# Hybrid attention and experts trunk, one core: the bias table laid out by position ahead of the launch, and the last experts in plain order

## What is computed

```python
for l in range(DEPTH):                                  # 2
    z = rms_norm(x, norm_mix[l]) @ w_in[l]              # 1024 x 3000
    ya = diff_attention(..., table[:, :4])              # 4 heads, two maps each
    yb = sparse_attention(..., table[:, 4:])            # 4 heads, the 64 best keys by an index score
    yc = mla(...)                                       # 4 heads, low-rank, no bias
    x = x + concat(ya, yb, yc) @ w_out[l]
    x = x + hier_moe(rms_norm(x, norm_ffn[l]), ...)     # 32 experts, each token goes to 2 of them
return rms_norm(x, norm_final)

def rel_bias(table, q0, n_keys):                        # table: 32 buckets x 8 heads, shared by the layers
    t, s = q0 + arange(128), arange(n_keys)
    return transpose(table[t5_bucket(s[None, :] - t[:, None])], (2, 0, 1))   # added to the logits
```

## Time and profile before

| | |
|---|---|
| runs | 1193.9, 1194.41, 1196.88 us; median 1194.41 |
| profiled execution | 1195.85 us; span 1194.0 us |
| busy | PE 933.0, PEld 583.0, DVE 334.3, ACT 196.0, POOL 18.4 us |
| DMA | 447.78 MB, mean 375 GB/s |
| granted TensorE clock | 0.903 of 2.4 GHz on the mean |
| chain that ended last | DMA 52%, PE 43%, ACT 1%, DVE 1%, issue 1% |

### The profile page before, as it was taken

One profiled execution on the slowest core, in us unless ns is written; L12 is line 12 of the kernel. 1 busy time (PEld: TensorE's weight loads), 2 busy tenths in 40 slices (PEclk: granted clock), 3 DMA queues, 4 the chain that ended last, 5 costly groups with the idle time before them and its releaser, 6 DMA issues.

```text
span 1194.0 us, 23281 instructions
## 1 busy us (share of the span) xinstructions
PE 933.0 (78%) x10312; PEld 583.0 (49%) x10317; DVE 334.3 (28%) x974; ACT 196.0 (16%) x529; POOL 18.4 (2%) x37
## 2 busy tenths in 40 slices
PE   9799999876667765776699999997776677648746
PEld 5577576443434343443368766664343334325423
DVE  3365662221102110211136465521111111111112
ACT  2134331010101010100022343311010001001102
POOL 1000000000000000000010000000000000000000
PEclk9899999898878788988799999999898888788878
DMA  8884499999999999999996165999999999999994
GB/s 322 358 305 139 186 375 424 425 431 429 427 432 425 431 426 431 424 430 430 423 426 226 63 260 213 388 427 431 428 429 425 432 427 430 429 428 427 429 431 176
DMA packets 35190, 447.78 MB, mean 375 GB/s; under 512 B 9584, under 2 KB 13072, under 8 KB 14992
## 3 DMA queue, kind: packets, MB, share of 16 engines
q1 hardware_dynamic: 32352, 443.49, 88.4%
q10 hardware_dynamic: 2736, 2.76, 0.7%
HBM read 442.57 MB, written 3.67 MB: 374 GB/s over the span
## 4 chain that ended last, share of the span: by engine, by line
DMA 52%; PE 43%; ACT 1%; issue 1%; DVE 1%; another core or an unknown queue 0%; POOL 0%; SPq 0%; ACTq 0%; POOLq 0%; DVEq 0%
DMA arena<-in_gate_up 22%; DMA xb<-in_w_down 14%; PE pv L1778 11%; PE pj L1399 7%; DMA ring<-in_w_down 7%; DMA ring<-in_gate_up 7%; PE tr L1800 5%; DMA bias_lines<-ring 2%; PE pj L1505 2%; PE pj L1405 2%; PE pj L1636 2%; PE pj L1810 2%; PE tr L1765 1%; PE pj L1611 1%; PE pj L1645 1%
## 5 line engine op out<-in xcount | busy, mean ns | idle before, releaser
L1778 PE MATMUL pv<-ring,xT 128*32 128x256 f32 x3072 | 222.4, 449 | 98.9 <-DMA ring<-in_gate_up 98.9
L1778 PEld LDWEIGHTS pv<-ring,xT 128*32 128x32 f32 x3072 | 107.8, 124 | 202.6 <-DMA ring<-in_gate_up 98.4
L1245 DVE TENSOR_SCALAR arena<-arena 128x128 f32<-128x128 f32 x64 | 14.5, 227 | 678.7 <-ACT arena L827 678.4
L1778 PE MATMUL pv<-arena,xT 128*32 128x256 f32 x1024 | 85.6, 502 | 67.6 <-DMA arena<-in_gate_up 67.6
L642 ACT ACTIVATE arena<-pv 128x256 f32<-128x256 f32 x64 | 24.5, 383 | 495.4 <-PE pv L1778 495.4
L1399 PE MATMUL pj<-xT,ring 128*128 128x256 f32 x448 | 101.9, 386 | 0.0
L1800 PE MATMUL tr<-ring,arena 128*32 128x256 f32 x1376 | 82.6, 380 | 15.0 <-issue 8.9
L1778 PEld LDWEIGHTS pv<-arena,xT 128*32 128x32 f32 x1024 | 39.0, 139 | 113.0 <-DMA arena<-in_gate_up 72.9
L1399 PEld LDWEIGHTS pj<-xT,ring 128*128 128x128 f32 x448 | 85.3, 193 | 13.7 <-issue 1.2
L1810 PE MATMUL pj<-arena 32*128 32x256 f32 x512 | 73.4, 403 | 8.1 <-ACT arena L642 8.1
L1810 PE MATMUL lg<-arena 32*128 32x256 f32 x512 | 73.4, 404 | 0.0
(11 more groups left out here) (238 smaller groups left out, 861.8 us busy)
## 6 DMA issues: line engine op xcount, KB each, us to landing
ring<-in_gate_up SPq DMA_DIRECT2D x42, 4096.0 KB, 48.5
ring<-in_w_down SPq DMA_DIRECT2D x40, 2048.0 KB, 41.3
arena<-in_gate_up SPq DMA_DIRECT2D x16, 4096.0 KB, 45.2
xb<-in_w_down SPq DMA_DIRECT2D x18, 2048.0 KB, 40.9
ring<-in_w_in_chunks SPq DMA_DIRECT2D x10, 2048.0 KB, 31.4
ring<-in_gate_up SPq DMA_DIRECT2D x10, 2048.0 KB, 8.7
ring<-in_w_out_halves SPq DMA_DIRECT2D x4, 2048.0 KB, 21.8
ring<-in_w_down SPq DMA_DIRECT2D x6, 1024.0 KB, 7.9
```

Of the source, the lines that this page charges most:

```text
L1778: ins = mm(gu_ps[i * CAP:(i + 1) * CAP, :], xg[:, j, c:c + CAP], w, start=(j == 0), stop=(j == KD - 1), tile_position=(0, i * CAP), skip_g ...
```

## The change

The bias is laid out by query and key for a tile of 128 queries ahead of the launch, as an input of 128 x 2048 numbers (`bias_rows`), like the weights, which already are laid out there. The kernel loads it in each layer on SP's queue between the input and output weights; GpSimd fills the masked corner in each layer; the one-hot matrix, the table product, the lines, their way through DRAM and the write-back are gone. In the last round of a layer, expert 30 is handled in the plain pattern, on TensorE and on ScalarE.

```diff
-    return (np.arange(REL_BUCKETS)[:, None] == bucket[None, :]).astype(np.float32)
+    return np.where(rel > 0, half, 0) + np.where(n < exact, n, np.minimum(large, half - 1))
 
 
 def loads_of(m):
...
-          gate_up_d, w_down, norm_final, consts_d, onehot_d, ffn_blocks_d, out_d):
-    lines_d = nc.dram_tensor("bias_lines", (8, P * LINE), F32, kind="Internal")
-    bias_d = nc.dram_tensor("bias_rows", (P, 8 * SEQ), F32, kind="Internal")
...
@@ -467,9 +457,6 @@
             def first_experts(l):
 
                 gu, down = gu_v[l * N_EXPERTS:], down_v[l * N_EXPERTS:]
-                if l < 1:
-                    sp.wait_ge(bias_ready, 1)
-                    sp.dma_start(bias_d[:, :], bias[:, 0:8, :].rearrange("p h k -> p (h k)")).then_inc(bias_out, 16)
                 sp.wait_ge(win_used[0], l + 1)
                 sp.wait_ge(win_used[1], l + 1)
                 sp.dma_start(gu_place[0], gu[0]).then_inc(gu_full[0], 16)
...
-                if l < 1:
-                    sp.wait_ge(bias_out, 16)
                 sp.dma_start(d_place[2][:, KE // 2:], down[2][:, KE // 2:]).then_inc(d_full[2], 16)
...
@@ -530,13 +515,9 @@
                         sp.dma_start(con[:, C_FIRST:], consts_d[:, C_FIRST:]).then_inc(more_consts_in, 16)
                     if l < 1 and i == 1:
                         load_small(sp, 0)
-                if l < 1:
-
-                    sp.wait_ge(lines_out, 16)
-                else:
-                    sp.wait_ge(bias_out, 16)
+                if l > 0:
                     sp.wait_ge(d_used[2], l * D_FILLS[2])
-                    sp.dma_start(bias[:, 0:8, :].rearrange("p h k -> p (h k)"), bias_d[:, :]).then_inc(bias_back, 16)
+                sp.dma_start(bias[:, 0:8, :].rearrange("p h k -> p (h k)"), bias_d[:, :]).then_inc(bias_in, 16)
                 for i in range(2):
                     if l > 0:
                         sp.wait_ge(d_used[1 - i], l * D_FILLS[1 - i])
...
                 rms_of(own, base, 3, 2, 6)
-                if l < 1:
-
-                    pool.wait_ge(bias_in, 16)
-                    nc.gpsimd.memset(bias[0:64, 0:8, SEQ - CHUNK:], NEG).then_inc(bias_ready, 1)
+                pool.wait_ge(bias_in, 16 * (l + 1))
+                nc.gpsimd.memset(bias[0:64, 0:8, SEQ - CHUNK:], NEG).then_inc(bias_ready, 1)
                 rms_of(own, base, 4, 6, 10)
...
-            act.dma_start(onehot, onehot_d).then_inc(tables_in, 16)
-            act.dma_start(table, rel_bias).then_inc(tables_in, 16)
...
-            def store_lines():
-
-                act.wait_ge(line_done, 1)
-                copy(lines, pv[:, 0, 0:LINE]).then_inc(line_copied, 1)
-                act.wait_ge(line_copied, 1)
-                act.dma_start(bass.AP(lines_d, 0, [[8 * LINE, P], [LINE, 8], [1, LINE]]), spread(lines, 1, 8)).then_inc(lines_out, 16)
-
-            def load_bias():
-
-                act.wait_ge(lines_out, 16)
-                act.dma_start(bias[:, 0:8, :], bass.AP(lines_d, P - 1, [[LINE - 1, P], [P * LINE, 8], [1, SEQ]])).then_inc(bias_in, 16)
...
-                if l == 0:
-                    act.wait_ge(tables_in, 32)
-                    copy(table_wide.rearrange("b (h c) -> b h c", h=8), spread(table, 2, P // 8)).then_inc(table_spread, 1)
...
-                if l == 0:
-                    store_lines()
...
-                if l == 0:
-                    load_bias()
                 act.wait_ge(lam_ready, at(l, 2, 1))
                 nc.scalar.activation(lam_exp, lam_dot, ACT.Exp).then_inc(lam_exped, 1)
                 dots_out(2); dots_out(3)
...
                     for e in range(1, BODY - 1):
-                        if m == ROUNDS - 1 and e == BODY - 2:
-                            y_out(e - 1)
-                            products_out(e)
-                        else:
-                            products_out(e)
-                            y_out(e - 1)
+                        products_out(e)
+                        y_out(e - 1)
                         exponent(e)
...
-                if l < 1:
-                    dve.wait_ge(bias_ready, 1)
-                else:
-                    dve.wait_ge(bias_back, 16)
+                dve.wait_ge(bias_ready, l + 1)
                 front(4); front(5); combine(4); combine(5); finish_pair(2)
...
-                if l == 0:
-                    pe.wait_ge(tables_in, 32)
-                    pe.wait_ge(table_spread, 1)
-                    mm(pv[:, 0, 0:LINE], table_wide, onehot, start=True, stop=True).then_inc(line_done, 1)
                 pe.wait_ge(xs_ready, at(l, TOK, TOK))
...
                 pe.wait_ge(tr_read, at(l, TR_EV, 6))
-                if l == 0:
-                    pe.wait_ge(line_copied, 1)
                 for t in range(TOK):
...
@@ -1906,16 +1851,10 @@
                     products(0)
                     turned(0)
                     for e in range(1, BODY - 1):
-                        early = m == ROUNDS - 1 and e == BODY - 2
-                        if early:
-                            down_of(e - 1)
-                            add(e - 1)
                         products(e)
-                        if not early:
-                            down_of(e - 1)
+                        down_of(e - 1)
                         turned(e)
-                        if not early:
-                            add(e - 1)
+                        add(e - 1)
                         if e == QUAD - 1:
                             tokens(1)
                     if m == ROUNDS - 1:
...
+    place = P - 1 - np.arange(P)[:, None] + np.arange(SEQ)[None, :]
+    a["bias_rows"] = a["rel_bias"][buckets()[place]].transpose(0, 2, 1).reshape(P, 8 * SEQ)
```

More of the change, by code:

```diff
@@ L112, in layer_constants, with buckets @@
     return c
-def bucket_one_hot():
+def buckets():
     rel = np.arange(LINE) - (SEQ - 1)
@@ L123, in bucket_one_hot @@
                      * np.float32(half - exact)).astype(np.int32)
-    bucket = np.where(rel > 0, half, 0) + np.where(n < exact, n, np.minimum(large, half - 1))
-    return (np.arange(REL_BUCKETS)[:, None] == bucket[None, :]).astype(np.float32)
+    return np.where(rel > 0, half, 0) + np.where(n < exact, n, np.minimum(large, half - 1))
 def loads_of(m):
@@ L203, in spread, with trunk @@
     return bass.AP(ap.tensor, ap.offset, pat)
-def trunk(nc, x_d, w_in_d, w_out_d, norm_mix, norm_ffn, rel_bias, lam_q1, lam_k1, lam_q2, lam_k2,
+def trunk(nc, x_d, w_in_d, w_out_d, norm_mix, norm_ffn, bias_d, lam_q1, lam_k1, lam_q2, lam_k2,
           diff_subln, mla_q_norm, mla_kv_norm, w_uq, w_ukv, w_group, b_group, w_expert, b_expert,
-          gate_up_d, w_down, norm_final, consts_d, onehot_d, ffn_blocks_d, out_d):
-    lines_d = nc.dram_tensor("bias_lines", (8, P * LINE), F32, kind="Internal")
-    bias_d = nc.dram_tensor("bias_rows", (P, 8 * SEQ), F32, kind="Internal")
+          gate_up_d, w_down, norm_final, consts_d, ffn_blocks_d, out_d):
     ctx = ExitStack()
@@ L348, in trunk @@
         rms_ps = lg[:, :, 0:P]
[L350 to L353, removed]
         win_full = [sem(f"win_full{i}") for i in range(len(WIN_CHUNKS))]
@@ L367, in trunk @@
         over_free = sem("over_free")
-        bias_out, bias_back, x_weighted, sums_open, rows_ready = sem("bias_out"), sem("bias_back"), sem("x_weighted"), sem("sums_open"), sem("rows_ready")
+        x_weighted, sums_open, rows_ready = sem("x_weighted"), sem("sums_open"), sem("rows_ready")
         sums_zeroed, upper_spent, upper_in = sem("sums_zeroed"), sem("upper_spent"), sem("upper_in")
         quarter_in, more_consts_in = [sem(f"quarter_in{i}") for i in range(2)], sem("more_consts_in")
-        consts_in, tables_in, lines_out, bias_in = sem("consts_in"), sem("tables_in"), sem("lines_out"), sem("bias_in")
+        consts_in, bias_in = sem("consts_in"), sem("bias_in")
         x_in = [sem(f"x_in{t}") for t in range(TOK)]
@@ L374, in trunk @@
             sem("xt_done"), sem("xt_read"), sem("diag_ready"), sem("rms_spread"), sem("xs_ready"))
-        line_done, line_copied, bias_ready = sem("line_done"), sem("line_copied"), sem("bias_ready")
-        table_spread = sem("table_spread")
+        bias_ready = sem("bias_ready")
         gain_in, small_in, final_in = sem("gain_in"), sem("small_in"), sem("final_in")
@@ L1968, in bcast_row @@
     return d[l].unsqueeze(0).to_broadcast([P, n])
-_INS = ["x", "w_in_chunks", "w_out_halves", "norm_mix", "norm_ffn", "rel_bias", "lam_q1", "lam_k1", "lam_q2", "lam_k2",
+_INS = ["x", "w_in_chunks", "w_out_halves", "norm_mix", "norm_ffn", "bias_rows", "lam_q1", "lam_k1", "lam_q2", "lam_k2",
         "diff_subln", "mla_q_norm", "mla_kv_norm", "w_uq", "w_ukv", "w_group", "b_group", "w_expert",
@@ L1995 @@
     arrays["const_table"] = layer_constants()
-    arrays["const_buckets"] = bucket_one_hot()
     arrays["ffn_blocks"] = np.ascontiguousarray(
```

## The result

The changed kernel takes 1181.65 us (median of 4 runs, 1179.70 to 1182.91), the one before 1194.85 (4 runs, 1193.90 to 1196.88): ratio 0.9886, 95% interval 0.9866 to 0.9905. Its profiled execution took 1182.24 us, span 1180.4. The forecast was 1178.0, range 1173 to 1186: the sign and the range held, and the gain was 13.2 us between the medians where 16.2 was forecast.

A forecast was written before the change was run, and what follows sets the result against it. It took the expert weight stream as the bound in the experts and TensorE's chain in attention. Gains of 11.4 and 4.8 us, 16.2 in sum, took the median from 1194.41 to 1178.2, said as 1178, range 1173 to 1186.

The forecast's parts named there:

- The stall: Layer 0's attention: without ScalarE's wait for the bias lines, TensorE's idle time and slow products go; 11.4 us gained.
- Rival B: Layer 0's attention: another wait steps in, only the 7.6 us of idle time come back; 1182.0 us, chance 0.10.
- E: Layer 0's attention gains nothing, the bias being late or its lines not the cause; 1190 us, chance 0.02.
- The bias transfer and GpSimd's memset: Attention of both layers: the bias load and masked-corner fill finish before their readers need them; cost 0.
- The end of layer 0: Last round: products(30) runs before down(29), products(31) at the lower clock; down(31) starts 3.4 us sooner.
- T: Landing of expert 29's down weights at a layer's end: 574.3 us in layer 0, 1159.3 in layer 1, before the change.
- The end of layer 1: Last round, the same new order and lower clock as in layer 0; down(31) starts 1.4 us sooner.
- if it falls, products(31) takes 2.0 more: End of each layer: if the clock falls, products(31) takes 5.8 us in place of 3.8; down(31) at T + 20.8.
- down(31) at 20 to 21 us after down 29's landing: Sign that the forecast is right: the start of down(31) in each layer, counted from T.
- rival A: Layer ends give nothing: expert 31's weights bind and the lower clock lasts through down(31); 1183 us, chance 0.13.
- D: After the idle stretch before products(31), the array stays at its lower clock to the layer's end; 1198 us, chance 0.02.
- 2.7 is nearest to 3.06, so I take the lower clock: Idle time before products(31): 2.7 us, judged by two rows, 3.83 us after 1.54 idle and 6.17 after 3.06.

The follow-up runs named there:

- e3: The kernel before with ScalarE's wait for the bias lines, and the read it guards, moved behind the last index products: 1187.06 us, ratio 0.9921.
- e8: The kernel before with 35 dummy products in TensorE's idle stretch in layer 0's attention: 1192.66 us, ratio 0.9977.
- e9: The changed kernel with four more copies of the bias rows per layer, DRAM to DRAM, behind the bias load: 1181.32 us, ratio 0.9898 against the kernel before.
- e1: The changed kernel with the old order of experts 29 and 30 put back: 1184.21 us, ratio 0.9912 against the kernel before.
- e4: The changed kernel with 24 dummy products instead of ten before products(31): 1179.69 us, ratio 0.9874 against the kernel before.
- e6: e4 measured a second time, beside a repeat of the changed kernel: 1179.63 us, ratio 0.9866 against the kernel before.
- e7: e4 with each layer's last down weights loaded in two halves, each with its own semaphore: 1178.13 us, ratio 0.9851 against the kernel before.
- e5: The changed kernel measured again, unchanged: 1180.70 us, ratio 0.9871 against the kernel before.
- e2: The kernel before with only the plain order of experts 29 and 30 in the last round: 1189.55 us, ratio 0.9956.
- e10: The changed kernel without the ten dummy products before products(31): 1181.33 us, ratio 0.9888 against the kernel before.

## Why the prediction was right, and where not

**The stall (11.4 forecast, 11.1 measured).** Right with its parts. Layer 1 as the template gave 145.00, and layer 0 came to 145.35. e3 shows the cause: the place of the wait, with the table product's 1.0 beside it as forecast. e8 shows the lower clock's 2.5 of the 2.8. So the return was 3.5 us more than the 7.6 us of idle time that the waits name, 1.0 of it the table product. Rival B is out, since no new wait of TensorE came, and so is E.

**The bias transfer and GpSimd's memset (0 forecast, 0 measured).** Right. The transfer took 28.1 us to land in layer 0 and 47.6 in layer 1, longer there than the 38.9 I used. The landing in layer 1 is 17.4 us after the second row projection, the turn 25.8; the logits come later still. e9 adds four times the bytes for nothing. One reason given for the zeros was wrong: the write of the lines (22 to 48 us) did not lie "where the stream is not full". A window of the kernel before, columns as in the earlier trace rows:

```profile
30.00:35.00 5.00, 5.00 (x29) 4.09 (x28) 0.70 (x2) 0.66 (x2) 0.00 (x0) 1.00 1.03 435
```

The stream was full there, and TensorE was busy all the same; the bytes cost nothing because no wait of TensorE hangs on them, as e3 and e9 show.

**The end of layer 0 (3.4 forecast, 3.1 measured).** With T taken 19.6 us behind products(29) as in the prediction, gate/up 31 came at T + 10.5 instead of T + 9.8, and down(31) 10.5 us behind products(31) instead of 11.0. The two errors nearly cancel, which is luck. One more thing was hidden in the trace of before: there products(30), behind down(29), took 4.88 us, in e1 with the same order 3.88. The two, before and e1:

```profile
580.66 4.88 PE L1778 MATMUL pv<-ring,xT 128*32 128x256 f32 x64
...
569.16 3.88 PE L1727 MATMUL pv<-ring,xT 128*32 128x256 f32 x64
```

E1's end 0 is 1.9 us shorter than that of before. Against e1 the order gives only 1.2 us in the traces (2.6 to 3.5 between the medians). So how much of the 3.1 us is the order's is not shown. Why the clock came back later in before, e3 and e8 than in e1 stays open.

**The end of layer 1 (1.4 forecast, 0 measured).** This is the term that was mis-sized. The step "if it falls, products(31) takes 2.0 more" was 2.6 here, since the lower clock lasted through two of the windows; and gate/up 31 came 0.6 later than "T + 9.8". Together down(31) stood at T + 22.0 where T + 20.8 was forecast, and T + 22.1 before. It lay inside the bounds (1.2 for the two ends at worst; its own terms, T + 22.6 twice, add up to 1.1). The sign "down(31) at 20 to 21 us after down 29's landing" held in layer 0 and failed in layer 1. The mechanism was right: the products wait after the dummies, the clock falls, and e4 and e6, which fill all or most of the wait, are 1.1 to 1.7 us shorter at each end than the changed kernel's traces (e7, with the halves too, 1.2 and 2.5). Of rival A the price came true at one end, but not its lower clock through down(31); D is out, as down(30) ran at 1.91 us in every trace.

**The clock over the gap.** "2.7 is nearest to 3.06, so I take the lower clock" gave the right answer for the changed kernel by a rule that does not hold; that too is luck. Idle time and then the time of products(31), over the traces: 1.76 and 3.86 us, 2.05 and 5.43 (both e9), 2.68 and 5.34, 3.35 and 6.45 (after), 2.69 and 5.30, 4.10 and 6.11 (e5), 3.35 and 3.85, 3.86 and 3.86 (e2), 5.17 and 5.35, 6.05 and 6.50 (e10). The two rows that the rule was read from the earlier trace rows were too few, too: the trace of before also has a product slow after a wait near the shorter of the two,

```profile
257.98 5.43 PE L1778 MATMUL pv<-ring,xT 128*32 128x256 f32 x64 [1.83 <-DMA ring<-in_gate_up]
```

The length of the wait alone does not decide. What does, no run here shows.

**What the 2.6 us between forecast and profiled execution (1179.7 and 1182.24) are made of.** 0.9 is the start: the second row projection starts between 14.29 and 15.66 us in the ten experiments, with and without the old bias work, so nothing shows it to be the change's. 0.3 is the stall, 0.3 the end of layer 0, 1.4 plus 0.15 the end of layer 1, and the two expert stretches give 0.45 back.

## What to carry to other kernels

A wait in an engine's program holds up whatever stands behind it. Look for the things behind it that another engine needs soon, and move the wait behind them before you rebuild what it waits for (e3 got 10 of the 11 us of the attention with one call moved). Price a stall with its clock: the idle time, plus what the products behind it take at the lower clock, best read from the same code running undisturbed elsewhere in the program. Dummy products that end before the data lands can be worth nothing; let them reach the landing, and then look for the next transfer in line, here the last one, which two halves hid.

## What the hardware showed that was not expected

- TensorE's granted clock stayed at 1.00 through 3.35 and 3.86 us of idle time (e2), while it fell after 2.68 us (after, 0.50 in the window of 575 to 578) and after 2.05 us (e9, 0.69 on the mean of 1154 to 1157), in the same place of the program.
- After it fell, products(31) took between 5.30 (e5) and 6.50 us (e10), and the down products behind them the usual 1.91. In the kernel before, after 9.95 us of idle time, the lower clock reached into a second group: down(29) 3.64, then products(30) 4.88 us.
- A 1.05 MB load on one queue took 28.1 us from issue to landing in layer 0, where four input chunks were issued in the 6.2 us before it, and 47.6 in layer 1, behind six chunks issued in the 14.5 us before it.
